# The order in which the columns of the 512-column products are read and written: last to first

## The reference

```python
def first_block(x, p, ...):
    hn = rmsnorm(h, mixer_norm[i])
    mix = gla_mixer(hn, gla_w_in[j], ..., gla_w_out[j])
    h = h + mix
    h = h + swiglu(rmsnorm(h, ffn_norm[i]), ffn_w_in[i], ffn_w_out[i])
    gate = jax.nn.sigmoid(jnp.einsum('btd,de->bte', rmsnorm(h, ple_norm[i]), ple_w_gate[i]))
    h = h + gate * jnp.einsum('btk,kd->btd', p[i], ple_w_proj[i])
    return rmsnorm(h, final_norm)

def second_block(x, ...):
    h = _rmsnorm(x, norm_pre_w[l])
    proj = jnp.einsum('bsd,de->bse', h, w_in[l])
    ...
    br_a = jnp.einsum('bsc,cd->bsd', y_a, w_proj_mlstm[l])
    br_b = jnp.einsum('bsc,cd->bsd', y_b, w_proj_pool[l])
    merged = jax.nn.sigmoid(g_a) * br_a + jax.nn.sigmoid(g_b) * br_b
    out = jnp.einsum('bsd,de->bse', merged, w_out[l])
    x = x + _rmsnorm(out, norm_post_w[l])
```

## Time and profile before

| | |
|---|---|
| median of three runs | 2200.72 us |
| profiled execution | 2200.2 us, of which the span from first to last instruction is 2198.5 us |
| TensorE matmul busy | 2188.7 us, 9954 records |
| VectorE / ScalarE / GpSimd busy | 1574.8 / 1082.1 / 19.8 us |
| mean granted TensorE clock | 1.000 |
| moved from HBM | 410.33 MB |

### The profile page before, as it was taken

The page is one execution under the profiler, slowest core; times in us unless marked ns, Lnnn a source line. Parts: engine busy times, 40 slices in busy tenths (PEclk is TensorE's granted clock), DMA queues, the critical chain, the costliest instruction groups (busy, mean ns, idle before and its releaser), DMA issues.

```text
span 2198.5 us, 27733 instructions
## 1 busy us (share of the span) xinstructions
PE 2188.7 (100%) x9954; PEld 1819.9 (83%) x9954; DVE 1574.8 (72%) x2395; ACT 1082.1 (49%) x1369; POOL 19.8 (1%) x41
## 2 busy tenths in 40 slices
PE   9999999999999999999999999999999999999998
PEld 8888888888888888888888888888888888888887
DVE  6887888877776457777778846889455559645875
ACT  5564554544444334444446545555445555443443
POOL 0000000000000000000000000000000000000000
PEclk9999999999999999999999999999999999999999
DMA  9654566666666666666666656666665556666663
GB/s 281 182 163 122 179 196 189 200 192 195 194 193 192 192 195 191 196 191 194 186 217 198 200 152 191 183 199 181 201 176 171 171 162 205 196 195 211 191 192 114
DMA packets 282925, 413.96 MB, mean 188 GB/s; under 512 B 21071, under 2 KB 145883, under 8 KB 282299
## 3 DMA queue, kind: packets, MB, share of 16 engines
q1 hardware_dynamic: 281806, 408.55, 61.9%
q10 hardware_dynamic: 1008, 3.94, 0.5%
HBM read 410.33 MB, written 2.10 MB: 188 GB/s over the span
## 4 chain that ended last, share of the span: by engine, by line
PE 99%; issue 0%; DMA 0%; DVE 0%; ACT 0%; DVEq 0%; POOLq 0%; POOL 0%; SPq 0%; ACTq 0%
PE acc L1314 31%; PE acc L1316 31%; PE acc L1315 31%; PE mx L1494 1%; PE mx L1535 0%; PE tp L1362 0%; DMA H<-in_x 0%; PE tp L1508 0%; PE tp L1507 0%; PE tp L1509 0%; PE mx L1291 0%; PE mx L1293 0%; PE mx L1292 0%; PE mx L1472 0%; PE tp L1552 0%
## 5 line engine op out<-in xcount | busy, mean ns | idle before, releaser
L1686 DVE TENSOR_TENSOR w_lo<-raw,w_hi 128x1024 fp32r<-128x1024 f32 (+1 forms) x769 | 934.9, 1219 | 524.5 <-ACT w_hi L801 520.7
L801 ACT CAST w_hi<-raw 128x1024 fp32r<-128x1024 f32 (+1 forms) x769 | 803.0, 1046 | 913.9 <-PE acc L1316 897.0
L1314 PE MATMUL acc<-w_hi,xa_hi 128*128 128x512 f32 x2228 | 874.8, 393 | 0.0
L1316 PE MATMUL acc<-w_hi,xa_lo 128*128 128x512 f32 x2228 | 867.4, 389 | 0.0
L1315 PE MATMUL acc<-w_lo,xa_hi 128*128 128x512 f32 x2228 | 867.2, 389 | 0.0
L1316 PEld LDWEIGHTS acc<-w_hi,xa_lo 128*128 128x128 f32 x2228 | 418.2, 188 | 87.8
L1314 PEld LDWEIGHTS acc<-w_hi,xa_hi 128*128 128x128 f32 x2228 | 418.5, 188 | 84.8
L1315 PEld LDWEIGHTS acc<-w_lo,xa_hi 128*128 128x128 f32 x2228 | 418.6, 188 | 84.2
L1314 PE MATMUL acc<-w_hi,xb_hi 128*128 128x512 f32 x384 | 149.6, 390 | 0.0
L1316 PE MATMUL acc<-w_hi,xb_lo 128*128 128x512 f32 x384 | 149.4, 389 | 0.0
L1315 PE MATMUL acc<-w_lo,xb_hi 128*128 128x512 f32 x384 | 149.4, 389 | 0.0
(11 more groups left out here) (313 smaller groups left out, 1240.4 us busy)
## 6 DMA issues: line engine op xcount, KB each, us to landing
raw<-in_w_in SPq DMA_DIRECT2D x192, 512.0 KB, 3.8
raw<-in_ffn_w_in SPq DMA_DIRECT2D x352, 256.0 KB, 2.9
raw<-in_gla_w_in SPq DMA_DIRECT2D x95, 512.0 KB, 4.0
raw<-in_ffn_w_out SPq DMA_DIRECT2D x88, 512.0 KB, 3.7
raw<-in_w_in SPq DMA_DIRECT2D x128, 256.0 KB, 3.0
raw<-in_gla_w_out SPq DMA_DIRECT2D x32, 512.0 KB, 4.1
raw<-in_ple_w_gate SPq DMA_DIRECT2D x32, 512.0 KB, 4.0
raw<-in_w_proj_mlstm SPq DMA_DIRECT2D x32, 512.0 KB, 3.7
```

The costliest lines, as they stand in the source:

```text
L801: nc.scalar.copy(w_hi[:, hl, 0:kc * job.w], raw[:, slot, 0:kc * job.w]).then_inc(hi_ready, 1)
L1314: nc.tensor.matmul(a[t][:, 0:w], xh, hi, start=first, stop=False)
L1316: ins = nc.tensor.matmul(a[t][:, 0:w], xl, hi, start=False, stop=last)
L1686: nc.vector.tensor_tensor(w_lo[:, hl, 0:kc * job.w], raw[:, slot, 0:kc * job.w], w_hi[:, hl, 0:kc * job.w].bitcast(F32), ALU.subtract) \
```

## The change

In the last branch of `product`, the one for 512 columns, the moving operand is given with its columns reversed (`hi[:, ::-1]`, `lo[:, ::-1]`), and so is the output (`a[t][:, 0:w][:, ::-1]`). Column 511 is read first and written first, column 0 last. The stationary operand, the order of the instructions, their counts and their waits stay. The branch for `ple_w_proj`, the one for 256 columns, the narrow ones and `opening_product` stay as they were.

```diff
                     for t in range(2) if only is None else (only,):
                         xh = xt_part(job, 0, k)[:, t * P:(t + 1) * P]
                         xl = xt_part(job, 1, k)[:, t * P:(t + 1) * P]
-                        nc.tensor.matmul(a[t][:, 0:w], xh, hi, start=first, stop=False)
-                        nc.tensor.matmul(a[t][:, 0:w], xh, lo, start=False, stop=False)
-                        ins = nc.tensor.matmul(a[t][:, 0:w], xl, hi, start=False, stop=last)
+                        to = a[t][:, 0:w][:, ::-1]
+                        nc.tensor.matmul(to, xh, hi[:, ::-1], start=first, stop=False)
+                        nc.tensor.matmul(to, xh, lo[:, ::-1], start=False, stop=False)
+                        ins = nc.tensor.matmul(to, xl, hi[:, ::-1], start=False, stop=last)
```

## The result

The changed kernel takes 2259.07 us (2258.51 to 2259.43, four runs) against 2200.95 (2200.11 to 2201.9): 58.1 us longer, a ratio of 1.0264 with a 95% interval of 1.0246 to 1.0281. I had forecast no change, 2200.7 us.

The account below looks back on a forecast made before the run. TensorE's matmul pitch was taken to bound the kernel. The terms summed to 9084 x 0 plus at most 0.3 us, giving a forecast median of 2200.7 us, with a range of 2150 to 2282 at 0.80.

Parts of the forecast that it names:

- What bounds the kernel: TensorE, busy 2188.7 of 2198.5 us: 9084 matmuls at a pitch of 226.7 ns, 94% of the span.
- Step 1: Moving operand read backwards in 9084 matmuls: cost between 0 and 8.8 ns each, taken as 0.
- Step 2: Output written backwards to the PSUM bank in 9084 matmuls: cost between 0 and 206 ns each, taken as 0.
- rival A: PSUM write or reader combines only ascending pairs: 206 ns on each of 9084 matmuls, about 4072 us; chance 0.17.
- Step 3: Fixed 13.3 ns per matmul goes with type and size of the stationary operand: gain taken as 0, bound -8 ns.
- Step 4: Direction changes between `opening_product` and `product` in the same banks: twice, at most 0.3 us, 0.01%.
- Step 5: ScalarE, VectorE and load queue only wait longer if the pitch grows, and follow if it shrinks a few per cent.
- B: Small cost per matmul from odd start or address generator going down: 2.5 to 8.8 ns, 2223 to 2280 us; chance 0.12.

Follow-up runs that it names:

- read_only: Against the kernel before, only the moving operand of L1314 to L1316 is read backwards, the bank written ascending: 2258.54 us, ratio 1.0262.
- others: L1314 to L1316 ascending as in the kernel before; operand and output of other matmuls reversed instead: 256-column `pool` job 118.2 ns for 120, plain float32 unchanged.
- columns: The three products with tiles cut to their first 128 to 448 columns, ascending or backwards by job; at 256 columns backwards is 1.6 ns faster.
- write_only: Against the changed kernel, the moving operand is read ascending again and only the bank is written backwards: 2200.18 us, ratio 0.9999 to the kernel before.
- swap4: The whole change, but with every four columns backwards inside ascending blocks, for operand and bank: 2200.51 us, ratio 1.0000 to the kernel before.
- pb: Job in a run giving each job its own order: blocks of 16 columns from last to first, ascending inside, operand and bank; 18 steps in 4.20 us.
- v2: Job in a run giving each job its own order: ascending blocks of 4 columns, each backwards inside, for operand and bank; 226.8 ns.
- blocks64: The whole change, but as eight blocks of 64 columns from last to first, ascending inside, for operand and bank: 2200.35 us, ratio 0.9998 to the kernel before.
- phase_x: The three products with the stationary operand's place shifted, or either operand replaced by repeated columns: 512 columns ascending 228.1 to 233.6 ns by shift in one job.

## Why the prediction was wrong

**What bounds the kernel.** Right, and it carried the result: 6.40 ns more on the mean step x 9084 is 58.1 us, and nothing absorbed any of it.

**Step 1, the read: the step that failed.** I priced it between 0 and 8.8 ns and took 0, because the neighbours stay adjacent and the run is long, "nearer to level 2 than to level 1". `read_only` shows 6.7 ns on each matmul, 58 us. The two rows I compared are plain float32 of 128 columns. `others` shows no cost of the direction for this type at 128 or 256 columns, and `columns` none for float32r at these widths: such rows couldn't show the cost. I had written for the write side that rows at half the rate prove nothing for the full rate, and didn't apply it to the read side. That the 6.7 lies below the upper bound is luck: blocks of 16 columns turned inside keep 15 of 16 neighbours adjacent, and cost 40 ns. Nothing in the trace of before could say 0 rather than 6.7.

**Step 2, the write.** Right by `write_only`: 0.9999. The fall to half the rate, rival A, didn't happen.

**Step 3, the fixed 13.3 ns.** It didn't go, as taken, but for a reason that isn't the one given. It doesn't go with the size of the stationary operand (229.6 ns at 64 columns), but all but 3 ns of it go when the moving operand is eight columns or fewer, repeated (216.5). So most of it goes with how the moving operand is read, though not all: it also moves with the place of the stationary one.

**Step 4, the change of direction.** Not seen: the total is explained without it.

**Step 5, everyone else.** Right: the waits rose by 73 and 50 us, and the 256-column rows stand still.

**The rivals.** B was right in kind and size, 2223 to 2280 against 2259, and had 0.12. Its reasons were the odd start, which `swap4` and `pb` refute, and a few cycles lost going down, which is nearer, though `v2` and `blocks64` show that going down costs only over a middle distance. Its prices, too, come from the earlier trace rows, so that they enclose 58 us is partly luck; its likeliest was the lower end, 23 us. Its own bar, that it counts from 0.48 ns on, should have given it more: with no row for the changed thing, a stretch of 0.5 ns around zero had been given five times the chance of everything between 0.5 and 9 ns. The range, 2150 to 2282, held the time only because it took B in.

**What stays open.** Why a falling stretch of eight columns or more costs, why the sum is eight cycles at 512 columns and nothing at 256, whether plain float32 would pay at 512, and what repeats with 16 columns. A stationary operand read in the other direction would tell whether it counts that the two operands are read in opposite directions; it wasn't tried. That both directions meet in one mechanism with the shifts of `phase_x` is a guess from their size, 233.4 backwards and at most 233.6 by the shift, and not shown.

No order tried that covers all 512 columns was faster than the ascending one, so none of these is a version to gain from.

## What to carry to other kernels

Where TensorE runs without a gap, a few nanoseconds on the pitch of a matmul are the whole effect: read the pitch over some 18 steps before and after, multiply by the count, and compare with the total before looking anywhere else. In this kernel a float32r moving operand of 512 columns is best read in rising order over stretches of 64 columns or more; a turn within four columns costs nothing, and neither did writing the bank backwards. This holds at the places that the operands have here: a stationary operand eight columns further on took the gain away. And a price read from rows at half the rate and a quarter of the width is no price for the full ones, for reads as little as for writes.

## What was not expected of the hardware

- Reading the moving operand (float32r, 512 columns) from the last column to the first costs 6.7 ns on 226.7; at 256 columns it gains 1 to 2 ns on 120; plain float32 at 256 and 128 columns shows no difference.
- Blocks of 16 columns turned inside take 266.6 ns, 18% more, while blocks of 4 are free and blocks of 8 and 32 cost 3%.
- Reading the same eight columns over and over takes 216.5 ns, ten less than reading 512 different ones; the same 16 take 241.
- The place of the stationary operand, eight columns further on, costs the ascending order 6.3 ns. The kernel before, at 226.7, doesn't pay this.
